# A hybrid retention, sparse attention and mixture-of-experts layer on one core: GpSimd's order in the expert loop

## The chip, the cores and the metric

The kernel runs on one core of one Trainium2 chip. The metric is the device time in microseconds of one execution.

## The reference, cut to what matters

One layer over 512 tokens of width 1024: RMS norm with an adaptive scale and shift, a projection, retention, sparse attention with its top-k choice, an output projection, and then the mixture of experts with which this change deals:

```python
top_vals, top_idx = lax.top_k(logits, TOP_K)              # 4 of 32 experts for each of 512 tokens
gates = jax.nn.softmax(top_vals, axis=-1)
xs = h[rows_tok]                                          # rows of each block's tokens, 128 a block
gu = xb @ w_gu[e] + b_gu[e]                               # 1024 -> 2048
gate, up = jnp.split(gu, 2, axis=-1)
gate = jnp.minimum(gate, 7.0); up = jnp.clip(up, -7.0, 7.0)
glu = gate * jax.nn.sigmoid(1.702 * gate)
ys = ((up + 1.0) * glu) @ w_down[e] + b_down[e]           # 1024 -> 1024
y = segment_sum(ys * gates, rows_tok)                     # back to the tokens
```

All tensors are float32. The weights of one expert are 8 MB (w_gu) and 4 MB (w_down). Of 128 rows in an expert's block some 64 are filled on average (512 x 4 / 32); an empty row has an index out of bounds, and the indirect DMA leaves it out.

## The kernel before

**Before the loop** the normed rows are stored to DRAM (`xn_rows`), and lists are made of which token (`tok_i`) and which output row (`dst_i`) stands in each place of each expert's block, one column per expert.

**The expert loop** has 32 items and runs on five engines at once, each with its own program and its own `Fori`; they meet by semaphores. It is pipelined by one item: period `i` (a round of `steady(i)`) does gate and up of expert `i` and then down of expert `i-1`.

- SyncE loads the weights in 12 chunks of 1 MB a period into a ring of six slots. It waits for a slot until `lo_ready` says that VectorE has read it.
- ScalarE rounds each chunk to a high part (`e_hi`, four buffers), VectorE subtracts to get the low part (`e_lo`, four buffers). A product is three matmuls: high by high, low by high, high by low. ScalarE waits for `chunk_used` of TensorE before it takes a buffer of e_hi anew.
- TensorE, in `steady(i)`: `act_turn` transposes the activations of expert i-1 (L1288), `gate_up` puts down the biases (L1299) and then 8 chunks of 12 matmuls (L1306 to L1308), then it waits for `gathered`, `x_turn` transposes the gathered rows of expert i+1 out of `xg` (L1280), and `down` does the bias (L1316) and 4 chunks of 12 (L1328 to L1330).
- After x_turn, ScalarE scales and splits the transposed rows (`x_parts`, L706 and L703), between chunks. VectorE clips gate and up (L1695, L1696), makes the product (L1700, L1703), the low part of the rows (L1475), and goes on with e_lo (L1468) of the next item. ScalarE writes the result of `down` to `ys` (`rows_out`, L703 `area<-bank`).
- GpSimd does what needs indices. `gather()` brings rows of `xn_rows` into `xg` (L629, one buffer); an indirect DMA scatters `ys` to `expert_rows` (L661). Each takes its indices from a column copied first (L647 to `gidx`, L659 to `sidx`). Two more small copies choose the row of biases for gate and up (`sel_g`) and for down (`sel_d`), both L634.

**GpSimd's order in period i**, which is written by hand: `bring(i)` waits until x_turn of item i is done and gather i has landed, gathers i+1, waits for `g_bias_used`, copies sel_g. `store(i)` waits for `d_bias_used`, copies sel_d, waits for ys (`y_ready`), scatters, and waits until that scatter has landed. So gather i+1 of period i is issued after the scatter at the end of round i-1, which is early in TensorE's period i.

An indirect DMA issued from GpSimd, the loads from SyncE: they are two queues, over the same 16 DMA engines. In the profile a tile `area` is a large buffer with many views in it: xg, ys, xgT and the activations among them. `xn_rows` is the DRAM tensor of normed rows.

**After the loop** an `If` handles blocks of more than 128 rows as further items, and then the rows are read back and summed with their gates.

Of the kernel before, what the change touches and what calls it, by code (L numbers as in the profile page):

```python
# [14 lines left out]
I32 = mybir.dt.int32  # L15
U32 = mybir.dt.uint32

P = 128
# [9 lines left out]
E = 32  # L28
# [67 lines left out]
def build(nc, x, c, ada_w, ada_b, norm1_g, w_in, mix_scale, w_o, norm2_g, router_w, router_b,  # L96
# [11 lines left out]
    with ctx:  # L108
        def sb(name, shape, dt=F32):
            return ctx.enter_context(nc.sbuf_tensor(name, shape, dt))  # L110

        def sem(name):
            return ctx.enter_context(nc.semaphore(name))
# [80 lines left out]
        after = dist[:, P:2 * P]  # L194
# [34 lines left out]
        sel_g, sel_d = sb("sel_g", [96, P], BF16), sb("sel_d", [96, P], BF16)  # L229
        gidx = sb("gidx", [P, 1], U32)  # L230
# [23 lines left out]
        g_vals, g_bias = ring[0:1, 4 * SLOT:5 * SLOT], ring[0:1, 5 * SLOT:6 * SLOT]  # L254


        routes = sb("routes", [P, 1728])
        hot = routes[:, 0:512].rearrange("p (n e) -> p n e", e=E)
        hotC = routes[:, 512:640].rearrange("p (n e) -> p n e", e=E)
        hot32 = routes[:, 1024:1152].rearrange("p (t e) -> p t e", e=E)  # L260
        tabT = routes[:, 1280:1408]
        tab = routes[:, 1408:1536]
        dstf, empty = routes[:, 1536:1584], routes[:, 1584:1632]
        dst_i, tok_i = routes[:, 1632:1680].bitcast(I32), routes[:, 1680:1728].bitcast(I32)

        consts_ready, late_consts = sem("consts_ready"), sem("late_consts")
        small_in, key_in, query_in = sem("small_in"), sem("key_in"), [sem("query_in0"), sem("query_in1")]
# [34 lines left out]
        gidx_ready, gathered = sem("gidx_ready"), sem("gathered")  # L302
        sidx_ready, scattered = sem("sidx_ready"), sem("scattered")
        sel_g_ready, sel_d_ready = sem("sel_g_ready"), sem("sel_d_ready")
        g_bias_used, d_bias_used = sem("g_bias_used"), sem("d_bias_used")
        xt_full, xt_taken, at_full = sem("xt_full"), sem("xt_taken"), sem("at_full")
# [238 lines left out]
        def _(pool):  # L545
# [82 lines left out]
            def gather():  # L628
                pool.indirect_dma_start(out=xg, out_offset=None, in_=xn2_dram,  # L629
                                        in_offset=bass.IndirectOffsetOnAxis(ap=gidx[:, 0:1], axis=0),  # L630
                                        bounds_check=last_token, oob_is_err=False).then_inc(gathered, 16)

            def choose_bias(sel, at, ready):
                pool.tensor_copy(sel[:], hot96[:, at].broadcast_to((96, P))).then_inc(ready, 1)  # L634

            pool.tensor_copy(gidx[:].bitcast(I32), tok_i[:, 0:1]).then_inc(gidx_ready, 1)
            pool.wait_ge(gidx_ready, 1)
            gather()
            pool.sem_clear(gidx_ready)
            choose_bias(sel_g, slice(0, 1), sel_g_ready)  # L640
            choose_bias(sel_d, slice(0, 1), sel_d_ready)

            def bring(i, nxt):

                pool.wait_ge(xt_full, i * 2 + 2)
                pool.wait_ge(gathered, i * 16 + 16)
                pool.tensor_copy(gidx[:].bitcast(I32), tok_i[:, nxt]).then_inc(gidx_ready, 1)  # L647
                pool.wait_ge(gidx_ready, 1)
                gather()
                pool.sem_clear(gidx_ready)  # L650
                pool.wait_ge(g_bias_used, i + 1)
                choose_bias(sel_g, nxt, sel_g_ready)

            def store(i, before, now):

                pool.wait_ge(d_bias_used, i)
                choose_bias(sel_d, now, sel_d_ready)
                pool.wait_ge(y_ready, i + 1)
                pool.tensor_copy(sidx[:].bitcast(I32), dst_i[:, before]).then_inc(sidx_ready, 1)  # L659
                pool.wait_ge(sidx_ready, 1)  # L660
                pool.indirect_dma_start(out=y_dram,  # L661
                                        out_offset=bass.IndirectOffsetOnAxis(ap=sidx[:, 0:1], axis=0),
                                        in_=ys, in_offset=None,
                                        bounds_check=last_row, oob_is_err=False).then_inc(scattered, 16)
                pool.sem_clear(sidx_ready)
                pool.wait_ge(scattered, i * 16)

            def opening(i):
                bring(i, slice(i + 1, i + 2))

            def steady(i):
                nxt, before, now = pool.snap(i + 1), pool.snap(i - 1), pool.snap(i + 0)
                bring(i, bass.ds(nxt, 1))
                store(i, bass.ds(before, 1), bass.ds(now, 1))

            def closing(i):
                store(i, slice(i - 1, i), slice(i, i + 1))

            opening(0)
            with pool.Fori(1, E) as i:  # L680
                steady(i)
            closing(E)
            n_over = pool.value_load(over_i[0:1, 16:17], min_val=0, max_val=OVER)
            with pool.If(n_over > 0):
                opening(E)
                with pool.Fori(E + 1, ITEMS) as i:
                    steady(i)
                closing(ITEMS)
# [4 lines left out]
        def _(a):  # L693
            steps = [0]

            def done(ins):

                steps[0] += 1
                ins.then_inc(act_step, 1)
                a.wait_ge(act_step, steps[0])  # L700
# [191 lines left out]
            def hi(period, c):  # L892

                a.wait_ge(*period.landed(c))
                if period.i is not first or c >= PARTS:
                    a.wait_ge(chunk_used, period.at(c) - (PARTS - 1))
                copy(e_hi[:, c % PARTS, :], raw(period.raw_slot(c))).then_inc(hi_ready, 1)

            def x_parts(i):

                for half in range(2):
                    a.wait_ge(xt_full, i * 2 + (half + 1))
                    for q in range(4):
                        k = 4 * half + q
                        last = affine(xgT[:, k, :], bank[6 + half][:, q * P:(q + 1) * P], a2[:, k:k + 1],
                                      modB[:, k:k + 1])
                    last.then_inc(xt_taken, 1)
                    a.wait_ge(xt_taken, i * 2 + (half + 1))
                    copy(x_hi[:, 4 * half:4 * half + 4, :], xgT[:, 4 * half:4 * half + 4, :]).then_inc(xhi_ready, 1)

            def act_parts(i):

                for half in range(2):
                    a.wait_ge(at_full, i * 2 + (half - 1))
                    copy(act_hi[:, 4 * half:4 * half + 4, :],
                         bank[6 + half].rearrange("p (k n) -> p k n", k=4)).then_inc(ahi_ready, 1)

            def sigmoid(i):
                a.wait_ge(gate_ready, i + 1)
                nc.scalar.activation(sg, gc, ACT.Sigmoid, scale=ALPHA).then_inc(sig_ready, 1)  # L920

            def rows_out():
                copy(ys, banks[:, 2048:3072]).then_inc(y_ready, 1)
# [3 lines left out]
            def opening(i):  # L927
                period, after = Opening(i), Later(i + 1)
                for c in range(PARTS, GU):
                    hi(period, c)  # L930
                sigmoid(i)
                x_parts(i + 1)
                for c in range(PARTS):
                    hi(after, c)

            def steady(i):
                period, after = Later(i), Later(i + 1)
                act_parts(i)
                for c in range(PARTS, CHUNKS):
                    hi(period, c)  # L940
                sigmoid(i)
                x_parts(i + 1)
                for c in range(3):
                    hi(after, c)
                a.wait_ge(chunk_used, i * CHUNKS + 8)
                a.wait_ge(sel_g_ready, i + 2)
                rows_out()
                hi(after, 3)

# [12 lines left out]
            nc.scalar.activation(gates[:], dgate[:], ACT.Exp).then_inc(gate_exp, 1)  # L962
            a.wait_ge(tables_ready, 1)
            opening(0)
            with a.Fori(1, E) as i:
                steady(i)
            closing(E)
            first = None
# [1 line left out]
            with a.If(n_over > 0):  # L970
                for c in range(PARTS):
                    hi(Opening(E), c)
                opening(E)
                with a.Fori(E + 1, ITEMS) as i:
                    steady(i)
                closing(ITEMS)
# [814 lines left out]
```

## Time and profile before

| what | value |
|---|---|
| median of 3 runs | 1724.37 us (1715.86, 1724.37, 1729.37) |
| the profiled execution | 1720.0 us, span 1718.2 us |
| TensorE busy | 1583.8 us (92%) |
| VectorE busy | 1386.1 us (81%) |
| ScalarE busy | 1130.4 us (66%) |
| GpSimd busy | 335.1 us (20%) |
| DMA | 478.98 MB, mean 279 GB/s |
| the chain that ended last | PE 48%, DMA 20%, DVE 11%, ACT 11%, issue 7%, POOL 3% |
| in it | DMA expert_rows<-area,sidx 10%, DMA area<-xn_rows,gidx 8% |

PE is TensorE, DVE is VectorE, ACT is ScalarE, POOL is GpSimd, SP is SyncE. The chain is followed back from the last instruction to what released each step, so its shares are time on the path, whereas the busy times of engines overlap. The matmuls are pipelined and a matmul's duration overlaps with its neighbours'; their rate is read from the starts.

### The profile page before, as it was taken

Reading aid. Unit: us, or ns where it says so; the run is one execution under the profiler, and the core shown is the slowest. Engines: PE = TensorE matmul, PEld = TensorE weight load, DVE = VectorE, ACT = ScalarE, POOL = GpSimd, SP = SyncE. Lnnn points to the kernel's source line nnn. Section 1 sums busy time; section 2 is a strip of 40 time slices with the busy share of each in tenths; the row PEclk is TensorE's granted clock in tenths of the full one; section 3 lists DMA queues with packets and bytes.
Section 4 is the critical chain, followed back from the end, with each engine's and each line's share of the span. In section 5 each row is a group of like instructions: output and inputs, shape, how many; then the busy total and the mean of one; then the engine's idle time right before and its main releaser. Section 6 shows DMA issues by size and latency. Waiting matters only on the chain.

```text
span 1718.2 us, 20912 instructions
## 1 busy us (share of the span) xinstructions
PE 1583.8 (92%) x7032; PEld 1244.9 (72%) x7032; DVE 1386.1 (81%) x1162; ACT 1130.4 (66%) x1173; POOL 335.1 (20%) x258
## 2 busy tenths in 40 slices
PE   3999989998699999999999999999999999999975
PEld 3678866745577878778787877878787787878762
DVE  4789934246589889898988989898898989889865
ACT  3544343324487877787787777788777778878751
POOL 1215200010102212221221222122223222211210
PEclk8999985597789999999999999999999999999997
DMA  9745210023578898998889999888989998898826
GB/s 350 229 141 201 98 62 1 0 80 123 211 298 334 333 358 347 352 357 344 324 338 359 344 362 355 350 330 335 363 340 364 350 349 335 342 346 340 347 106 254
DMA packets 97712, 478.98 MB, mean 279 GB/s; under 512 B 24264, under 2 KB 33584, under 8 KB 45360
## 3 DMA queue, kind: packets, MB, share of 16 engines
q1 hardware_dynamic: 86848, 456.76, 69.8%
q0 software_dynamic: 10832, 21.81, 3.5%
q8 instruction: 18, 0.29, 0.1%
q14 instruction: 14, 0.11, 0.0%
HBM read 474.84 MB, written 20.98 MB: 289 GB/s over the span
## 4 chain that ended last, share of the span: by engine, by line
PE 48%; DMA 20%; DVE 11%; ACT 11%; issue 7%; POOL 3%; POOLq 0%; ACTq 0%; SPq 0%; DVEq 0%
DMA expert_rows<-area,sidx 10%; DMA area<-xn_rows,gidx 8%; PE bank L1307 6%; PE bank L1306 6%; PE bank L1308 6%; ACT e_hi L703 5%; PE bank L1328 4%; PE bank L1329 4%; PE bank L1330 4%; ACT area L706 3%; PE bank L1190 2%; PE bank L1135 2%; POOL sidx L659 2%; PE bank L1156 2%; DVE w_lo L1429 1%
## 5 line engine op out<-in xcount | busy, mean ns | idle before, releaser
L1468 DVE TENSOR_TENSOR e_lo<-ring,e_hi 128x2048 fp32r<-128x2048 f32 x384 | 872.5, 2293 | 120.6 <-ACT e_hi L703 117.8
L703 ACT ACTIVATE e_hi<-ring 128x2048 fp32r<-128x2048 f32 x384 | 732.7, 1920 | 218.9 <-PE bank L1308 198.9
L1306 PE MATMUL bank<-e_hi,x_hi 128*128 128x512 f32 x1024 | 407.5, 398 | 1.5 <-DVE e_lo L1468 1.5
L1307 PE MATMUL bank<-e_lo,x_hi 128*128 128x512 f32 x1024 | 404.0, 395 | 0.0
L1308 PE MATMUL bank<-e_hi,x_lo 128*128 128x512 f32 x1024 | 402.8, 393 | 0.0
L1306 PEld LDWEIGHTS bank<-e_hi,x_hi 128*128 128x128 f32 x1024 | 193.5, 189 | 48.5 <-DVE e_lo L1468 2.4
L1307 PEld LDWEIGHTS bank<-e_lo,x_hi 128*128 128x128 f32 x1024 | 193.4, 189 | 42.1
L1308 PEld LDWEIGHTS bank<-e_hi,x_lo 128*128 128x128 f32 x1024 | 193.2, 189 | 41.6
L1328 PE MATMUL bank<-e_hi,act_hi 128*128 128x512 f32 x512 | 210.8, 412 | 4.9 <-DVE act_lo L1481 4.9
L1329 PE MATMUL bank<-e_lo,act_hi 128*128 128x512 f32 x512 | 203.8, 398 | 0.0
L1330 PE MATMUL bank<-e_hi,act_lo 128*128 128x512 f32 x512 | 203.3, 397 | 0.0
L703 ACT ACTIVATE area<-bank 128x1024 f32<-128x1024 f32 (+5 forms) x90 | 59.9, 665 | 153.0 <-PE bank L1023 68.0
L1328 PEld LDWEIGHTS bank<-e_hi,act_hi 128*128 128x128 f32 x512 | 97.5, 191 | 31.4 <-DVE act_lo L1481 5.4
L1330 PEld LDWEIGHTS bank<-e_hi,act_lo 128*128 128x128 f32 x512 | 97.4, 190 | 23.6
L1329 PEld LDWEIGHTS bank<-e_lo,act_hi 128*128 128x128 f32 x512 | 97.6, 191 | 22.7
L706 ACT ACTIVATE area<-bank,modB,a 128x128 f32<-128x128 f32 x264 | 98.4, 452 | 18.8 <-PE bank L1280 18.7
L659 POOL COPY sidx<-routes 128x1 int32 (+1 forms) x32 | 37.5, 1172 | 374.3 <-ACT area L703 374.3
L634 POOL COPY sel_d<-hot 96x128 bf16 (+1 forms) x33 | 32.2, 976 | 313.1 <-PE bank L1316 310.7
L647 POOL COPY gidx<-routes 128x1 int32 (+1 forms) x32 | 39.7, 1241 | 258.9 <-DMA expert_rows<-area,sidx 230.4
L1280 PE MATMUL bank<-ident,area 128*128 128x128 f32 x264 | 37.7, 289 | 41.3 <-DMA area<-xn_rows,gidx 41.3
L578 POOL TENSOR_TENSOR area<-ring,area 128x2048 f32<-128x2048 f32 x10 | 48.5, 4859 | 134.8 <-ACT ring L703 127.5
L1280 PEld LDWEIGHTS bank<-ident,area 128*128 128x128 f32 x264 | 31.8, 148 | 50.2 <-issue 43.4
(245 smaller groups left out, 1996.2 us busy)
## 6 DMA issues: line engine op xcount, KB each, us to landing
ring<-in_w_gu SPq DMA_DIRECT2D x256, 1024.0 KB, 6.4
ring<-in_w_down SPq DMA_DIRECT2D x128, 1024.0 KB, 6.9
ring<-in_ada_w SPq DMA_DIRECT2D x24, 1024.0 KB, 7.3
ring<-in_w_in SPq DMA_DIRECT2D x9, 1024.0 KB, 6.1
ring<-expert_rows SPq DMA_DIRECT2D x6, 1024.0 KB, 10.7
ring<-in_w_o SPq DMA_DIRECT2D x4, 1024.0 KB, 7.4
ring<-in_w_in SPq DMA_DIRECT2D x10, 256.0 KB, 5.2
xs<-in_x SPq DMA_DIRECT2D x4, 512.0 KB, 5.1
```

Of the source, the lines that this page charges most:

```text
L578: nc.gpsimd.tensor_tensor(o, slot(LOAD_B[n]), o, ALU.add).then_inc(rest_used[half], 1)
L659: pool.tensor_copy(sidx[:].bitcast(I32), dst_i[:, before]).then_inc(sidx_ready, 1)
L703: return nc.scalar.activation(dst, src, ACT.Copy, scale=scale)
L706: return nc.scalar.activation(dst, src, ACT.Identity, scale=scale, bias=bias)
L1280: mm = pe.transpose(bank[6 + half][:, q * P:(q + 1) * P], xg[:, k * P:(k + 1) * P], ident[:])
L1306: pe.matmul(bank[b][:], x_hi[:, c, :], hi, start=False, stop=False)
L1307: pe.matmul(bank[b][:], x_hi[:, c, :], lo, start=False, stop=False)
L1308: mm = pe.matmul(bank[b][:], x_lo[:, c, :], hi, start=False, stop=(c == GU - 1))
L1328: pe.matmul(bank[4 + q][:], act_hi[:, kk, :], hi, start=False, stop=False)
L1329: pe.matmul(bank[4 + q][:], act_hi[:, kk, :], lo, start=False, stop=False)
L1330: mm = pe.matmul(bank[4 + q][:], act_lo[:, kk, :], hi, start=False, stop=(kk == KD - 1))
L1468: tt(e_lo[c % PARTS][:], raw(period.raw_slot(c)), e_hi[:, c % PARTS, :].bitcast(F32), ALU.subtract).then_inc(lo_ready, 1)
```

## The change

In GpSimd's program the gather of an item is put behind the transposes that empty `xg`: round i now chooses sel_g, waits for x_turn of item i+1, and gathers item i+2; the first two gathers stand before the loop. The wait for a landed scatter at the end of `store` goes; GpSimd waits for the scatter before only where it overwrites `sidx`, and ScalarE waits for it before it overwrites `ys` (where it waited for sel_g). Since the last rounds read two columns ahead, the list of tokens has eight more columns, which are set to zero before the first gather. The first round is written out on GpSimd and ScalarE, as it has no scatter to wait for.

```diff
-        routes = sb("routes", [P, 1728])
+        routes = sb("routes", [P, 1736])
...
-        dst_i, tok_i = routes[:, 1632:1680].bitcast(I32), routes[:, 1680:1728].bitcast(I32)
+        dst_i, tok_i = routes[:, 1632:1680].bitcast(I32), routes[:, 1680:1736].bitcast(I32)
...
-            pool.tensor_copy(gidx[:].bitcast(I32), tok_i[:, 0:1]).then_inc(gidx_ready, 1)
-            pool.wait_ge(gidx_ready, 1)
-            gather()
-            pool.sem_clear(gidx_ready)
-            choose_bias(sel_g, slice(0, 1), sel_g_ready)
-            choose_bias(sel_d, slice(0, 1), sel_d_ready)
-
-            def bring(i, nxt):
-
-                pool.wait_ge(xt_full, i * 2 + 2)
-                pool.wait_ge(gathered, i * 16 + 16)
+            done(nc.gpsimd.memset(tok_i[:, 48:56], 0))
+
+            def take_rows(nxt):
+
                 pool.tensor_copy(gidx[:].bitcast(I32), tok_i[:, nxt]).then_inc(gidx_ready, 1)
                 pool.wait_ge(gidx_ready, 1)
                 gather()
                 pool.sem_clear(gidx_ready)
+
+            take_rows(slice(0, 1))
+            choose_bias(sel_g, slice(0, 1), sel_g_ready)
+            choose_bias(sel_d, slice(0, 1), sel_d_ready)
+            pool.wait_ge(xt_full, 2)
+            pool.wait_ge(gathered, 16)
+            take_rows(slice(1, 2))
+
+            def bring(i, nxt, after):
+
                 pool.wait_ge(g_bias_used, i + 1)
                 choose_bias(sel_g, nxt, sel_g_ready)
+                pool.wait_ge(xt_full, i * 2 + 4)
+                pool.wait_ge(gathered, i * 16 + 32)
+                take_rows(after)
 
             def store(i, before, now):
 
                 pool.wait_ge(d_bias_used, i)
                 choose_bias(sel_d, now, sel_d_ready)
                 pool.wait_ge(y_ready, i + 1)
+                if i is not 1:
+                    pool.wait_ge(scattered, (i - 1) * 16)
                 pool.tensor_copy(sidx[:].bitcast(I32), dst_i[:, before]).then_inc(sidx_ready, 1)
...
                 pool.sem_clear(sidx_ready)
-                pool.wait_ge(scattered, i * 16)
 
             def opening(i):
-                bring(i, slice(i + 1, i + 2))
+                bring(i, slice(i + 1, i + 2), slice(i + 2, i + 3))
 
             def steady(i):
-                nxt, before, now = pool.snap(i + 1), pool.snap(i - 1), pool.snap(i + 0)
-                bring(i, bass.ds(nxt, 1))
+                if i is 1:
+                    bring(1, slice(2, 3), slice(3, 4))
+                    store(1, slice(0, 1), slice(1, 2))
+                    return
+                after, nxt = pool.snap(i + 2), pool.snap(i + 1)
+                before, now = pool.snap(i - 1), pool.snap(i + 0)
+                bring(i, bass.ds(nxt, 1), bass.ds(after, 1))
                 store(i, bass.ds(before, 1), bass.ds(now, 1))
 
             def closing(i):
                 store(i, slice(i - 1, i), slice(i, i + 1))
+                pool.wait_ge(scattered, i * 16)
 
             opening(0)
-            with pool.Fori(1, E) as i:
+            steady(1)
+            with pool.Fori(2, E) as i:
                 steady(i)
...
                 a.wait_ge(chunk_used, i * CHUNKS + 8)
-                a.wait_ge(sel_g_ready, i + 2)
+                if i is not 1:
+                    a.wait_ge(scattered, (i - 1) * 16)
                 rows_out()
                 hi(after, 3)
...
             opening(0)
-            with a.Fori(1, E) as i:
+            steady(1)
+            with a.Fori(2, E) as i:
                 steady(i)
```

## Rows read from the trace of the kernel before

**Rows 1.** Busy times by stretch: length, busy of each engine, PEclk, DMA share, GB/s.

```profile
516.50:1651.70 1135.20, 1098.16 (x4982) 890.86 (x4981) 1025.35 (x601) 893.75 (x781) 249.97 (x180) 0.99 0.89 344
896.10:935.20 39.10, 36.52 (x168) 29.50 (x167) 36.62 (x22) 30.80 (x27) 10.47 (x6) 1.00 0.90 357
935.20:971.50 36.30, 36.30 (x168) 29.58 (x167) 31.75 (x20) 28.82 (x26) 6.91 (x6) 1.00 0.91 339
```

**Rows 2.** Waits, 516.5 to 1651.7: total us, times, longest.

```profile
POOL gidx L647 <- DMA expert_rows<-area,sidx: 230.4, 30, 9.2
ACT e_hi L703 <- PE bank L1308: 183.8, 225, 0.9
...
PE bank L1280 <- DMA area<-xn_rows,gidx: 37.0, 15, 2.8
```

**Rows 3.** The chain, 896 to 923: start, us, what.

```profile
896.93 1.02 ACT area L703
898.10 2.09 POOL sidx L659
900.48 11.13 DMA expert_rows<-area,sidx
912.20 1.26 POOL gidx L647
913.73 8.78 DMA area<-xn_rows,gidx
```

**Rows 4.** TensorE's timeline at four places: start, us, what, idle before.

```profile
922.63 1.09 PE L1280 MATMUL bank<-ident,area 128*128 128x128 f32 x8 [2.58 <-DMA area<-xn_rows,gidx]
...
958.98 1.04 PE L1280 MATMUL bank<-ident,area 128*128 128x128 f32 x8
...
971.45 1.11 PE L1288 MATMUL bank<-ident,area 128*128 128x128 f32 x8
...
973.08 0.59 PE L1306 MATMUL bank<-e_hi,x_hi 128*128 128x512 f32 x1
```

**Rows 5.** Busy times by stretch, two of four with PEclk at 0.50.

```profile
543.10:546.50 3.40, 3.32 (x12) 2.80 (x13) 3.40 (x4) 3.19 (x7) 0.35 (x1) 0.50 1.01 424
...
1526.10:1529.50 3.40, 3.40 (x10) 2.63 (x9) 3.37 (x3) 3.34 (x10) 1.89 (x1) 0.50 1.09 414
```

**Rows 6.** The gathers of L629, from issue to landing.

```profile
DMA to landing us min/median/max: 4.3/8.5/10.5
```

**Rows 7.** VectorE's timeline from 968.85.

```profile
968.85 6.70 DVE L1468 TENSOR_TENSOR e_lo<-ring,e_hi 128x2048 fp32r<-128x2048 f32 x3
```

**Rows 8.** DMA, 516.5 to 1651.7: all, and the instruction queue.

```profile
DMA packets 60193, 390.72 MB, mean 344 GB/s; under 512 B 10637, under 2 KB 10637, under 8 KB 14368
...
q14 instruction: 1, 0.01, 0.0%
```

**Rows 9.** Busy times by stretch, two with the DMA queues loaded.

```profile
898.00:930.00 32.00, 29.41 (x133) 23.81 (x132) 29.80 (x19) 25.26 (x24) 10.47 (x6) 1.00 1.00 404
934.00:964.00 30.00, 30.00 (x140) 24.50 (x139) 25.35 (x15) 21.88 (x18) 6.91 (x6) 1.00 0.97 363
```

**Rows 10.** Waits of SyncE's DMA queue, 516.5 to 1651.7.

```profile
SPq L478 <- DVE e_lo L1468: 629.3, 233, 6.3
```

**Rows 11.** GpSimd's timeline at the first gather.

```profile
428.79 0.18 POOL L636 COPY gidx<-routes 128x1 int32<-128x1 int32 x1 [18.89 <-DVE routes L1661]
429.56 2.95 POOL L629 DMA_INDIRECT area<-xn_rows,gidx  x1 [0.59 <-POOL gidx L636]
```

**Rows 12.** GpSimd's groups before 480: busy us, mean ns, idle before.

```profile
L615 POOL MEMSET area<- 128x1024 f32 x1 | 1.0, 970 | 0.0
```

**Rows 13.** GpSimd's groups, 516.5 to 1651.7.

```profile
L629 POOL DMA_INDIRECT area<-xn_rows,gidx x30 | 40.7, 1357 | 9.2 <-POOL gidx L647 9.2
L647 POOL COPY gidx<-routes 128x1 int32 x30 | 38.8, 1295 | 230.4 <-DMA expert_rows<-area,sidx 230.4
```

**Rows 14.** All instructions of VectorE's line 1468: ns min/median/max.

```profile
L1468 DVE TENSOR_TENSOR e_lo<-ring,e_hi x384: 2278/2292/2378, 429.2 to 1655.7; 128x2048 fp32r<-128x2048 f32 x192
```

## The prediction

> **What bounds the kernel now.** I read the stretches first, then the waits, then the chain, then single timelines. The expert loop from period 2 to period 31 takes 1135.20 of the 1718.2 us span [rows 1]. A period here runs from one transposition of the activations (L1288) to the next; there are 30 of them in that stretch, 37.84 us each on average. They are not alike. The third row of [rows 1] is one in which TensorE is busy all 36.30 us. The second is its neighbour: 39.10 us with the same 168 matmuls and 36.52 us busy. So a period of 36.30 us is what TensorE itself needs at full clock, and everything over it is waiting.
>
> The waits say on whom [rows 2]. In these 30 periods TensorE has one kind of wait only: the transposes of the next expert's rows (L1280) wait for the gather, 15 times, 37.0 us in all. It waits for no e_lo and no DMA of weights there. ScalarE waits for TensorE (183.8 us over 225 times, to get an e_hi buffer back), and the GpSimd queue has 230.4 us of waiting for a scatter to land before it copies the next indices.
>
> The chain through one slow period gives the order [rows 3]. ys is written at 896.93, GpSimd copies the scatter's indices (2.09 us), the scatter takes 11.13 us from its issue to its landing, the loop's last line waits for it, then come the copy of the gather's indices and the gather itself, 8.78 us. It lands at 922.5, and the transposes start at 922.63, 2.58 us late [rows 4]. The gather needs nothing of the scatter: its buffer xg was emptied by the transposes one period earlier. It stands behind it only in GpSimd's program. In the other period of a pair scatter and gather are quicker and the transposes (958.98) start without any wait [rows 4]. That is why it is 15 of 30.
>
> A stall costs twice where the clock falls. [...] At half speed 3.4 us hold 1.7 us of work: 4 x 1.7 = 6.8 us.
>
> **The change part by part.**
>
> *The gather moves to right behind the transposes.* In period i, GpSimd now waits for the transposes of rows i+1 (the end of L1280), copies indices and gathers rows i+2. Those are read by the transposes of the next period. From rows: transposes end at 960.0 (958.98 + 1.04) [rows 4]; the index copy is at most about 2.1 us (the sidx copy of [rows 3], nearest of its size), and a gather landed 4.3 to 10.5 us after its issue [rows 6]. That gives landing at most 13 us after the transposes, and it is wanted 36.30 - 1.04 = 35.3 us after. Some 22 us are to spare, so no ordinary delay brings the wait back. What goes: 30 x 36.30 = 1089.0 us in place of 1135.20, that is **-46.2 us**. The terms agree: 37.0 us of waits, 6.8 us of clock, and 2.4 us left, 0.16 for each of the 15 stalls, the start of PE's pipeline after a stop.
>
> *The scatter's wait moves to its users.* ScalarE waits for scatter i-1 before it writes ys, and GpSimd before it overwrites sidx. That scatter was issued at about 4 us into the period and landed by 16 us (900.48 + 11.13, against 896.1) [rows 3]; ys is next written at 36.30 + 0.8 us. 20 us to spare: 0 us. ScalarE loses its wait for sel_g, which never ended last in [rows 2]: 0 us. If the gather in the same queue held the scatter up by a whole gather (10.5 us), 9 us would still be left.
>
> *GpSimd's queue.* Per period it issues what it did: four small copies and two indirect DMAs. Behind its new wait for the transposes stand the gather, sel_d, and the scatter. sel_d is wanted by `down` of the next period, 30 us later; the scatter's ys comes 12 us after the transposes (971.45 against 958.98) [rows 4], while gather issue plus copies are 2.1 + 3.0 + 2.1 us at the most. sel_g is chosen before the wait, about 7 us into the period, wanted at its end. 0 us.
>
> *What is late next.* The chain of the next expert's first e_lo. In the period without a wait VectorE makes e_lo of the next chunks 0 to 2 in one run from 968.85, 2.23 us each [rows 7], so chunk 0 is there at 971.1; the matmul that reads it starts at 973.08 [rows 4]. Margin 2.0 us. That period has this margin already at full pace, and its neighbours met it too, so two in a row need nothing new. VectorE works 1025.35 us in the stretch [rows 1], 34.2 per period, 94% of 36.30: near, not over.
>
> *The transfers.* The stretch moves 390.72 MB [rows 8]. In 1089.0 us that is 359 GB/s, now 344. Over 32 us the same queues moved 404 GB/s at a share of 1.00, and in the period without a wait 363 GB/s at 0.97, which is 374 at a full share [rows 9]. 359 is under both. SP's queue waits for e_lo to free a slot 233 times with 629.3 us for w_gu alone [rows 10]: loads are held back by slots, not by the engines. Cost 0, cover about 4% in the worse of the two rows.
>
> *Before the loop.* A memset of 128x8 with a wait of its own comes between the ready lists and the first gather, which is on the path (TensorE waits for that gather). There GpSimd took 0.18 us for a copy of that size and 0.59 us to the next [rows 11]; a memset of 128x1024 took 0.97 us [rows 12]. Between 0.2 and 2.1 us (a copy that met VectorE, [rows 3]); I take **+0.6 us**, as the short copy and a wait are nearest. Once more GpSimd gathers at the very end (34 gathers for 33), for a list that is not used; nothing waits for it: 0 us. The peeled first rounds on GpSimd and ScalarE lengthen the code and repeat no work. The instruction queue moved one packet in all 30 periods [rows 8], so a loop's code is not fetched anew each round: 0 us, at most the 2.1 us of a short stall, once.
>
> **Sum.** 1720.0 (the profiled execution, span 1718.2) - 46.2 + 0.6 = 1674.4 us. The profiled execution is 4.4 us below the median of 1724.37. If that difference is in the stalls, it goes with them; if it is elsewhere, it stays (1678.8). I say 1675.
>
> **Rivals.**
>
> *GpSimd gets in VectorE's way (1694).* The copy of the indices (mean 1.30 us) and the gather's issue (1.36 us) [rows 13] now fall beside VectorE's clip, swiglu and x_lo, the chain with 2.0 us of margin. Were VectorE held for both, 2.66 - 2.0 = 0.66 us are lost per period; 30 x 0.66 = 20, so 1694. (Over 2.0 + 1.54 us of holding a period, 1.54 being 46.2 / 30, the gain would be gone.) Against it: the longest of 384 e_lo instructions took 2378 ns with a median of 2292 [rows 14], though GpSimd's copies and issues fell beside many of them. It is GpSimd that waits: its copies of one column take 0.18 or 2.09 us [rows 3, 11]. [...] I give this 5%.
>
> *The transfers don't keep up (slower, 1737).* With no stalls left, the ring of six slots gets no periods in which to catch up, and gather and scatter lie close together: one in the last 10 us of a period, the other in the first 14. If the queues then deliver only 339 GB/s, which is what the period without a wait shows as a whole [rows 1], a period takes 13.02 MB / 339 = 38.4 us, 2.1 more, and the whole 1674.4 + 63 = 1737. It decides from 344 GB/s down, where all the gain is gone, and below 338 (a period of 38.55 us) the time is over 1742. For it: 339 there, and share 0.91. Against: that row includes time in which SP had no free slot, and where the queues had work they gave 363 to 404. 5%.
>
> *Nothing changes (1720).* The transposes would have to be held by something that merely ends with the gather, or the clock would fall without stalls. [rows 2] names the gather in all 15, and [rows 5] are all at a wait. 5%.
>
> **The numbers.** The forecast has 83%, the three rivals 15%, other things 2%. A measurement of this kernel tells about 1% from no change, 1707 to 1742. Faster by over 1%: 0.83 + 0.05 (VectorE held) + 0.02 = 0.90. Within 1%: 0.05 from nothing changes and 0.02 from transfers between 338 and 350 GB/s, 0.07. Slower: 0.03, transfers below 338. The low end is the sum less the spread of the runs (1715.86 against 1724.37 is 8.5): 1666. The high end takes in 1678.8 and the VectorE case: 1695.
>
> **What would show it.** In the profile after: no wait of L1280 for the gather between periods 2 and 31, periods of 36.30 us throughout, granted clock 1.00 over that stretch, its length 1089 us, DMA share about 0.93. GpSimd's idle time before the gidx copy is ended by TensorE (L1280), not by the scatter. Wrong would be: an idle before L1306 ended by e_lo (the margin of 2.0 us is gone), ScalarE's e_hi waiting for a DMA (transfers), ys waiting for the scatter, or half-clock stretches inside the loop without a stall.

## The result: 1675.68 us, as forecast, and the profile after

The changed kernel takes 1675.68 us (median of 4 runs, 1674.71 to 1678.61) against 1726.87 us for the kernel before on the same chip: a ratio of 0.9694, interval 0.9651 to 0.9736. A run over 1.5% above the fastest of its kernel counts as slow: two runs of the kernel before do in the later sessions, two of the version held to 5 chunks (experiment 2) and one of that held to 6. The profiled execution is 1675.41 us with a span of 1673.6 us. Forecast: 1675, range 1666 to 1695.

The stretches, from the first transposition of period 2 to that of period 32, and one period (length, busy of PE, PEld, DVE, ACT, POOL, granted clock, DMA share, GB/s):

```profile
518.50:1607.50 1089.00, 1089.00 (x4982) 887.31 (x4981) 1020.04 (x601) 888.78 (x781) 255.47 (x180) 1.00 0.91 359
881.50:917.80 36.30, 36.30 (x168) 29.58 (x167) 34.00 (x21) 29.62 (x27) 8.51 (x6) 1.00 0.93 363
```

Against [rows 1]: 1089.00 us for 1135.20, TensorE busy all of it, the clock at 1.00 throughout. All 30 periods are 36.30 us, where there were 15 of 36.3 and 15 of 38.7 to 40.8. The DMA share is 0.91, where the prediction looked for 0.93. The waits of that stretch (total us, times, longest):

```profile
POOL gidx L640 <- PE bank L1296: 478.8, 30, 16.0
POOL sidx L667 <- ACT area L717: 338.0, 30, 11.3
ACT e_hi L717 <- PE bank L1324: 174.0, 210, 0.9
DVE e_lo L1484 <- ACT e_hi L717: 63.7, 150, 0.5
```

TensorE is in no row. The 230.4 us in which GpSimd waited for its scatter before a gather [rows 2] are now 478.8 us in which it waits for the transposes: more idle time than before, and none of it on the path. The chain that ended last says the same by shares:

```profile
PE 84%; DVE 9%; ACT 3%; DMA 2%; issue 1%; SPq 0%; DVEq 0%; POOLq 0%; POOL 0%; ACTq 0%
```

It was PE 48% and DMA 20%; the two indirect DMAs (10% and 8%) have gone out of it. GpSimd's timeline of one period, which begins at 881.5 (start, us, what, idle before):

```profile
883.59 2.01 POOL L667 COPY sidx<-routes 128x1 int32 x1 [11.28 <-ACT area L717]
885.87 2.77 POOL L669 DMA_INDIRECT expert_rows<-area,sidx  x1 [0.28 <-POOL sidx L667]
888.65 1.97 POOL L634 COPY sel_g<-hot 96x128 bf16 x1
906.57 0.42 POOL L640 COPY gidx<-routes 128x1 int32 x1 [15.96 <-PE bank L1296]
907.26 1.04 POOL L629 DMA_INDIRECT area<-xn_rows,gidx  x1 [0.27 <-POOL gidx L640]
908.31 0.30 POOL L634 COPY sel_d<-hot 96x128 bf16 x1
```

The gather is issued 25.8 us into the period and is wanted 34 us later, since the transposes stand 23.8 us into the next one (958.98 against 935.20 in [rows 1, 4]). It takes 3.8 to 8.6 us to land, where it took 4.3 to 10.5 [rows 6]:

```profile
DMA to landing us min/median/max: 3.8/7.5/8.6
```

What is outside the loop: the first gather. The last step of the list before it, in the chain of before and of after, and then GpSimd's timeline after:

```profile
428.31 0.19 DVE routes L1661
```

```profile
430.06 0.19 DVE routes L1677
```

```profile
430.50 0.10 POOL L636 MEMSET routes<- 128x8 int32 x1 [18.85 <-DVE routes L1677]
430.67 0.18 POOL L640 COPY gidx<-routes 128x1 int32<-128x1 int32 x1
431.32 2.94 POOL L629 DMA_INDIRECT area<-xn_rows,gidx  x1 [0.46 <-POOL gidx L640]
```

The list was ready 1.75 us later in this execution, before any changed instruction (and 5.43 us later, at 433.93, in the one of experiment 6). From the end of that step to the gather's issue it is 1.07 us (430.25 to 431.32), with the memset's 0.10 in it, and before it was 1.06 (428.50 to the 429.56 of [rows 11]).

### The profile page after: what moved, and what is told of

It is laid out like the page before. It is cut to its first block, busy times and chain, and to the rows that moved or that the text cites. A ratio compares the mean times of both kernels' runs of the same rounds, so it can differ in the third digit from the quotient of the medians.

```text
span 1673.6 us, 20929 instructions
## 1 busy us (share of the span) xinstructions
PE 1574.7 (94%) x7032; PEld 1241.6 (74%) x7032; DVE 1379.7 (82%) x1162; ACT 1125.2 (67%) x1173; POOL 343.2 (21%) x261
## 4 chain that ended last, share of the span: by engine, by line
PE 84%; DVE 9%; ACT 3%; DMA 2%; issue 1%; SPq 0%; DVEq 0%; POOLq 0%; POOL 0%; ACTq 0%
PE bank L1323 14%; PE bank L1324 14%; PE bank L1322 14%; PE bank L1344 7%; PE bank L1346 7%; PE bank L1345 7%; PE bank L1206 3%; PE bank L1151 2%; PE bank L1172 2%; PE bank L1304 2%; PE bank L1315 2%; PE bank L1296 2%; DVE w_lo L1445 2%; DMA ring<-in_ada_w 1%; PE bank L1159 1%; PE bank L1037 1%
## 5 line engine op out<-in xcount | busy, mean ns | idle before, releaser
L1323 PE MATMUL bank<-e_lo,x_hi 128*128 128x512 f32 x1024 | 404.1, 395 | 0.0
L1323 PEld LDWEIGHTS bank<-e_lo,x_hi 128*128 128x128 f32 x1024 | 193.4, 189 | 42.2
L667 POOL COPY sidx<-routes 128x1 int32 (+1 forms) x32 | 62.6, 1956 | 364.2 <-ACT area L717 364.2
L640 POOL COPY gidx<-routes 128x1 int32 (+1 forms) x34 | 14.2, 418 | 533.2 <-PE bank L1296 533.1
L669 POOL DMA_INDIRECT expert_rows<-area,sidx x32 | 86.8, 2713 | 9.0 <-POOL sidx L667 9.0
L634 POOL COPY sel_g<-hot 96x128 bf16 (+1 forms) x33 | 62.9, 1906 | 11.1 <-PE bank L1315 11.0
L1560 DVE SCALAR_TENSOR_TENSOR area<-area,bank 128x128 f32<-128x128 f32 (+3 forms) x32 | 15.6, 487 | 51.5 <-PE bank L1151 51.5
```

What stands on the lines that cost most here:

```text
L669: pool.indirect_dma_start(out=y_dram, out_offset=bass.IndirectOffsetOnAxis(ap=sidx[:, 0:1], axis=0), in_=ys, in_offset=None, bounds_check= ...
L1323: pe.matmul(bank[b][:], x_hi[:, c, :], lo, start=False, stop=False)
```

## The experiments

All were timed in 3 rounds against the kernel before on the same chip, whose medians were 1727.67, 1725.28 and 1724.28 us in the three sessions. Each edit is shown against the changed kernel.

**1. Which half of the change did it.** The gather moved, the scatter's wait kept where it was:

```diff
                 pool.sem_clear(sidx_ready)
+                pool.wait_ge(scattered, i * 16)
```

> The changed kernel, but GpSimd still waits at the end of each round for its scatter to land. Theory (the gather was late only because it stood behind the scatter): the wait now ends about 15.5 us into the period, before sel_g (wanted at 36) and before the transposes of the next rows (25), so nothing moves: 1675 us, all 30 periods 36.30. Rival (the removed scatter wait was the real cause): back to 1720.

1676.77 us, ratio 0.9709 (0.9655 to 0.9764). The rival falls. GpSimd does wait for its scatter again, 30 times, but now before sel_g, where nobody is waiting:

```profile
POOL sel_g L634 <- DMA expert_rows<-area,sidx: 256.7, 30, 9.4
```

So 256.7 us of waiting for a scatter cost nothing in this place of the program, whereas 230.4 us of such waiting [rows 2] stood in front of the gather before.

The other half alone: the gather stays in its old place, behind the scatter's issue, and only the wait between them is gone.

```diff
-            pool.wait_ge(xt_full, 2)
-            pool.wait_ge(gathered, 16)
-            take_rows(slice(1, 2))
...
             def bring(i, nxt, after):
 
+                pool.wait_ge(xt_full, i * 2 + 2)
+                pool.wait_ge(gathered, i * 16 + 16)
+                take_rows(nxt)
                 pool.wait_ge(g_bias_used, i + 1)
                 choose_bias(sel_g, nxt, sel_g_ready)
-                pool.wait_ge(xt_full, i * 2 + 4)
-                pool.wait_ge(gathered, i * 16 + 32)
-                take_rows(after)
```

> Only the scatter's wait is moved; the gather keeps its old place, right behind the scatter's issue in GpSimd's program. Theory: scatter issued by 7.2 us into the period, index copy up to 2.1, gather issued at about 9.5 and landed 7.5 to 10.5 later, 17 to 20 us, wanted at 23.8: no wait either, 1675 us. Rival (the gather has to stand behind the transposes; two indirect DMAs of one queue follow each other whole): the gather starts when the scatter has landed, as before, and the time stays at 1720.

1673.94 us, ratio 0.9693 (0.9639 to 0.9748): the whole gain again. GpSimd's timeline, in a period that begins at 877.8 (start, us, what, idle before):

```profile
879.95 2.00 POOL L664 COPY sidx<-routes 128x1 int32 x1 [12.68 <-ACT area L714]
882.23 2.77 POOL L666 DMA_INDIRECT expert_rows<-area,sidx  x1 [0.28 <-POOL sidx L664]
885.00 1.87 POOL L640 COPY gidx<-routes 128x1 int32 x1
887.14 1.04 POOL L629 DMA_INDIRECT area<-xn_rows,gidx  x1 [0.27 <-POOL gidx L640]
```

and the gathers' time from issue to landing:

```profile
DMA to landing us min/median/max: 4.3/9.7/10.7
```

The gather is issued at 9.3 us, behind a scatter in flight, and lands by 20.0 at the latest, 3.8 before it is wanted at 23.8. Either half is enough; the two do not add.

**2. How late may the gather be.** From the version just shown, the gather is also held until gate and up of the current expert have used 3, 5 or 6 chunks (the line for 5):

```diff
                 pool.wait_ge(gathered, i * 16 + 16)
+                if i is not 0:
+                    pool.wait_ge(chunk_used, i * CHUNKS + 1)
                 take_rows(nxt)
```

> The gather held until gate and up have used 3 chunks, 10.2 us into the period. Theory (36.30 plus what the landing is later than 23.8): lands at 10.3 + 1.4 + 0.3 + 8.3 = 20.3 on the mean and at 22.3 with the longest landing seen (10.7): 1675 us, no wait. With the runs held to chunks 5 and 6 that makes a knee between. Rival (holding GpSimd's program behind chunks costs by itself): over 1700.

> As the run with the wait moved only, and the gather is held until gate and up of the current expert have used 5 chunks, 15.8 us into the period. Theory (a period costs 36.30 plus what the landing is later than 23.8): copy 0.4 to 2.1, 0.3, landing 7.5: 24.0 to 25.7, so 0.2 to 1.9 us of wait, 0.16 for the restart, 31 times: 1686 to 1739, middle 1712. Rival (the gather isn't what counts): 1675.

> As before, held to 6 chunks, 18.6 us into the period: 2.79 us more in each of 31 periods, so 86 us over the run held to chunk 5 if the clock stays (about 1798), and up to 1.7 x 31 = 53 us on top if the granted clock falls at every wait (about 1850). A slope of less than 2.79 us a period would say that something else than the gather's landing ends the wait.

Held to 3: 1675.72 us, ratio 0.9728 (0.9701 to 0.9754), all periods 36.30. Held to 5: 1768.97 us (1740.40 to 1787.08), ratio 1.0272 (1.0191 to 1.0353), above the range of 1686 to 1739. Against the kernel before that leaves open whether it is slower by over 2%. Against the same version without the hold, timed in the same session (experiment 1, second half, 1671.52 to 1678.36), every run is at least 62 us longer. Held to 6: 1889.95 us (1875.22 to 1903.95), ratio 1.0912 (1.0810 to 1.1015), above the 1850. The knee is where it was expected, the loss behind it is larger. TensorE's waits in the 30 periods, first held to 5, then to 6:

```profile
PE bank L1295 <- DMA area<-xn_rows,gidx: 50.6, 25, 3.5
```

```profile
PE bank L1295 <- DMA area<-xn_rows,gidx: 131.5, 30, 5.9
```

and the loop's stretches, in the same order:

```profile
514.90:1673.40 1158.50, 1107.81 (x4982) 894.96 (x4982) 1024.46 (x600) 895.63 (x780) 221.24 (x180) 0.99 0.88 336
```

```profile
528.30:1817.00 1288.70, 1157.18 (x4985) 933.02 (x4985) 1033.02 (x601) 904.46 (x781) 178.54 (x180) 0.94 0.81 302
```

Held to 6, the 30 gaps before the transposes are 4.4 us each, close to the 4.8 that 18.6 + 1.4 + 0.3 + 8.3 - 23.8 gives, and 2.7 us more than held to 5, where 2.79 was expected. So the gather's landing ends the wait, as the theory says. What the expectation had too small is the clock. It was at 0.50 in 29 pieces, 160 us together, which is up to 80 us of lost work (part of it lies in the gaps, where nothing is lost twice); gaps and clock together make the 199 us over 1089. The expectation had one piece of 3.4 us a wait at the most, the length of those in [rows 5]; 18 of the 29 were of 6.8. Held to 5, gaps of 51 us and half of the 31 us at a granted clock of 0.50 make 66 of the 69 over 1089, and 0.16 for each of 25 waits about the rest (what the 0.16 is stands with the loop's term below). That expectation's range held no term for the clock. All this is the profiled execution, the fastest of four at 1740.40; no trace shows where the other three lost up to 47 us more.

**3. VectorE's margin.** One or two more products of 128x1024 behind swiglu, ahead of x_lo and the next e_lo; their result is not used (the lines for two; the semaphore's declaration is left out).

```diff
                 tt(act, uc, sg, ALU.mult).then_inc(act_ready, 1)
+                for k in range(2):
+                    tt(uc, uc, sg, ALU.mult).then_inc(more_ready, 1)
+                    v.wait_ge(more_ready, i * 2 + (k + 1))
```

> The changed kernel with one more 128x1024 product on VectorE per item, behind swiglu, in the chain that makes the next item's first e_lo (its result is not used). Theory (that chain has 2.0 us of margin): 1.23 us and some 0.1 for its own wait fit in, 36.30 us a period, 1675 us. Rival (VectorE at 94% of the period is as good as full): 1.3 us a period, 31 x 1.3 = 40, 1715 us.

> The same with two more products, 2.6 us. Theory: 0.6 us over the margin in each of 31 periods, 19 us: 1694 us, with TensorE's wait before L1322 ended by e_lo; if these waits make the granted clock fall, up to 1.7 us each on top. Rival (full already): 31 x 2.6 = 81, 1756 us.

One: 1674.64 us, ratio 0.9689 (0.9625 to 0.9754), periods 36.30. Two: 1690.72 us, ratio 0.9785 (0.9719 to 0.9850), periods of 36.74 with one gap, before the first L1323, ended by e_lo:

```profile
PEld bank L1323 <- DVE e_lo L1485: 18.7, 29, 0.6
```

0.44 us a period where 0.6 was expected, and 30 x 0.44 = 13 of the 16 us between the two medians. So the margin is 2.1 to 2.2 us, near the 2.0 read from [rows 4, 7], and the granted clock stayed at 1.00 with these waits. VectorE was busy 1067.50 of 1087.00 us there:

```profile
520.00:1607.00 1087.00, 1082.63 (x4910) 872.87 (x4909) 1067.50 (x650) 874.57 (x764) 241.48 (x176) 1.00 0.89 357
```

98% busy cost 0.44 us a period, and 97% with one product none. Here the busy share did not say when VectorE begins to hold others up; the margin in one chain did.

**4. GpSimd beside VectorE.** Four copies of 128x512 behind each gather's issue:

```diff
                 gather()
                 pool.sem_clear(gidx_ready)
+                for k in range(4):
+                    pool.tensor_copy(future[:], dist[:]).then_inc(gidx_ready, 1)
+                    pool.wait_ge(gidx_ready, k + 1)
+                pool.sem_clear(gidx_ready)
```

> The changed kernel with four copies of 128x512 on GpSimd right behind each gather's issue, SBUF to SBUF, beside VectorE's clip, swiglu, x_lo and e_lo. Theory (GpSimd is the one that waits): each copy takes up to 2.3 us in the trace, VectorE's e_lo stays at 2291 ns median and under 2400, the time at 1675 us. [...]

1674.73 us, ratio 0.9684 (0.9619 to 0.9748): no time lost. But the theory's sentence that VectorE is untouched is wrong: the longest e_lo in the 30 periods took 2643 ns. GpSimd's four copies in one period (start, us, what):

```profile
909.67 0.62 POOL L645 COPY future<-dist 128x512 f32<-128x512 f32 x1
```

```profile
910.36 0.61 POOL L645 COPY future<-dist 128x512 f32<-128x512 f32 x1
```

```profile
911.04 2.55 POOL L645 COPY future<-dist 128x512 f32<-128x512 f32 x1
```

```profile
913.65 1.49 POOL L645 COPY future<-dist 128x512 f32<-128x512 f32 x1
```

VectorE's timeline beside them:

```profile
909.36 1.22 DVE L1716 TENSOR_SCALAR area<-bank 128x1024 f32<-128x1024 f32 x1
910.49 2.63 DVE L1488 TENSOR_TENSOR e_lo<-ring,e_hi 128x2048 fp32r<-128x2048 f32 x1
913.04 1.62 DVE L1720 SCALAR_TENSOR_TENSOR area<-area 128x1024 f32<-128x1024 f32 x1
914.70 1.52 DVE L1723 TENSOR_TENSOR area<-area 128x1024 f32<-128x1024 f32 x1
```

and the same four without them, in the changed kernel:

```profile
908.00 1.21 DVE L1712 TENSOR_SCALAR area<-bank 128x1024 f32<-128x1024 f32 x1
909.13 2.28 DVE L1484 TENSOR_TENSOR e_lo<-ring,e_hi 128x2048 fp32r<-128x2048 f32 x1
911.33 1.22 DVE L1716 SCALAR_TENSOR_TENSOR area<-area 128x1024 f32<-128x1024 f32 x1
912.58 1.23 DVE L1719 TENSOR_TENSOR area<-area 128x1024 f32<-128x1024 f32 x1
```

The three instructions with two inputs in SBUF (e_lo and the two products) are 0.3 to 0.4 us longer each, 1.0 us together, less than the margin of 2.1. On the mean of 30 periods the two products take 1.63 and 1.52 us against 1.22 and 1.23. The clip, which reads a bank, is as long as before, and the copies beside it take 0.61 and 0.62 us, near the 568 ns of an iota of that size. The third copy begins while e_lo runs and ends at 913.59, 0.47 us behind the end of e_lo (913.12); the fourth ends 0.48 us behind the end of the first product (914.66). So of the 2.55 and 1.49 us that they took, all but 0.47 and 0.48 lie beside VectorE's instruction, where a whole copy took 0.61 beside the clip. The other way round, each of the three VectorE instructions began 0.44 to 0.55 us before the end of a copy that was running, and is longer by a little less than that. In these five meetings both sides were held: what came second took longer by about the time that the other still ran. That VectorE can be held by GpSimd, as the prediction's rival has it, is shown here, and with it how little it costs: three VectorE instructions of a period met a copy, and each lost 0.3 to 0.4 us, what was left of the copy and not all of it.

**5. The transfers' margin.** One or two more loads of 1 MB a period in SyncE's queue, to a spare DRAM tensor that nobody reads (the line for two):

```diff
                     gu_chunk(period, c, e)
+                    if c in (3, 6):
+                        sp.dma_start(spare[i, (c % 2) * P:(c % 2 + 1) * P, :], w_gu[e, c * P:(c + 1) * P, :]).then_inc(spare_in, 16)
```

> The changed kernel with one more load of 1 MB per period in SyncE's queue, from w_gu to a spare DRAM tensor (not used). 14.06 MB a period, 387 GB/s at 36.30 us. Theory (the queues can do 374 to 404 at a full share): between no loss (404) and 37.6 us a period (374), so 1675 to 1715, middle 1690. Rival (the transfers were already the limit at 359): 13.02 to 14.06 MB is 8% of 36.30, 2.9 us a period, 31 x 2.9 = 90, 1765.

> The same with 2 MB more, 15.1 MB a period, 416 GB/s at 36.30 us, over both rows. Theory: the queues bound the period, 15.1 MB / 404 = 37.4 us to 15.1 / 374 = 40.4: 31 x 1.1 to 4.1 = 34 to 127 more, 1709 to 1802, and ScalarE's e_hi waits for a DMA. Rival (limit already at 359): 42.1 us a period, 1855.

One: 1677.25 us, ratio 0.9738 (0.9716 to 0.9759), periods of 36.30. Two: 1697.11 us, ratio 0.9848 (0.9824 to 0.9871), below the range. All the DMA of 520 to 1607, with one and with two:

```profile
DMA packets 61113, 420.81 MB, mean 387 GB/s; under 512 B 11161, under 2 KB 11161, under 8 KB 14835
```

```profile
DMA packets 61039, 445.81 MB, mean 410 GB/s; under 512 B 11395, under 2 KB 11395, under 8 KB 15069
```

and with two, ScalarE's waits and the loads' median time to landing (6.8 us in the changed kernel):

```profile
ACT e_hi L721 <- DMA ring<-in_w_gu: 108.1, 31, 4.6
ACT e_hi L721 <- DMA ring<-in_w_down: 54.7, 96, 0.9
```

```profile
ring<-in_w_gu SPq DMA_DIRECT2D x234, 1024.0 KB, 11.6
```

The limit is a little above the better of the expectation's two rows (404): 410 GB/s at a share of 0.99, and 15.1 MB / 410 = 36.9 us against the 37.0 us that the periods take from the ninth on; periods 2 to 8 still take 36.30. So the changed kernel has a cover of 410 / 359, 14%, not 4%. The extra loads go from DRAM to DRAM; whether loads into SBUF alone reach 410 is not shown.

**6. The memset.** Put ahead of the wait for the lists:

```diff
+            done(nc.gpsimd.memset(tok_i[:, 48:56], 0))
             pool.wait_ge(xn2_stored, 16 * T)
             pool.wait_ge(lists_ready, 1)
...
-            done(nc.gpsimd.memset(tok_i[:, 48:56], 0))
```

> The changed kernel with the memset of the eight new columns put ahead of the wait for the lists. Both theories: within the noise in time (1675 us). In the trace the memset (0.10 us and about 0.07 to the copy behind it) leaves the path to the first gather: gidx copy 0.2 us sooner after the list is ready than the 0.27 us shown with the memset. The 0.6 us of the prediction for it would be too much.

1675.68 us, ratio 0.9688 (0.9623 to 0.9753). GpSimd's timeline there:

```profile
434.23 0.18 POOL L640 COPY gidx<-routes 128x1 int32<-128x1 int32 x1 [18.79 <-DVE routes L1677]
435.00 2.93 POOL L630 DMA_INDIRECT area<-xn_rows,gidx  x1 [0.58 <-POOL gidx L640]
```

and the last step of the list in the same run:

```profile
433.74 0.19 DVE routes L1677
```

From the end of that step to the copy it takes 0.30 us, and 0.42 with the memset in between (430.25 to 430.67): 0.12 sooner, where 0.2 was expected. To the gather's issue it is 1.07 us either way, so the memset costs the gather nothing. The medians show no version faster than the changed kernel by more than the spread of its runs.

## Why the prediction was right

**What bounds it.** Right. The 15 waits for the gather (37.0 us [rows 2]), with a granted clock of 0.50 for 3.4 us behind each of four of them [rows 5] (from about 543, 847, 1526 and 1601 us), were what stood over 36.30 us, and moving the gather's landing in three steps moved the time with it, with a knee between 3 and 5 chunks (experiment 2).

**The loop, -46.2 us.** 1135.20 - 1089.00 = 46.20, measured. The terms of the kernel before add up to it: 37.0 us of waits, 4 x 1.7 = 6.8 us for the clock, and 15 x 0.16 = 2.4. The 0.16, which the prediction put down to the start of PE's pipeline, is how the profile counts a wait. The last matmuls before the wait of 2.58 us in [rows 4] (start, us, what):

```profile
919.42 0.40 PE L1307 MATMUL bank<-e_lo,x_hi 128*128 128x512 f32 x1
919.65 0.39 PE L1308 MATMUL bank<-e_hi,x_lo 128*128 128x512 f32 x1
```

They start 0.23 us apart and last 0.39 to 0.40, and a wait is counted from the end of the last, so some 0.16 us more than the wait is lost. That a period without a wait can follow another was argued from its margin, and it does.

**The scatter's wait, 0.** Right as said: scatter and ys need nothing sooner. What the prediction did not see is that this part alone would have brought the whole gain (experiment 1). It priced the two parts as a cause (the gather's place) and a thing without cost (the wait), where either is enough.

**The front, +0.6.** The mis-sized term: 0.01 us by the trace (1.07 against 1.06). The size was taken from a copy and the 0.59 us behind it; that gap stands before the issue of the indirect DMA in the kernel before too [rows 11], and was 0.46 after. The 2.1 us that the prediction allowed once for a short stall by the longer code is its author's guess: no run shows such a stall, and the 30 periods of 36.30 us hold none.

**The sum.** Span: 1718.2 - 46.2 + 2.0 - 0.4 = 1673.6. Of the 2.0, 1.75 came before the changed code, and the 0.4 lies behind the loop. With the 1.8 between span and time that is the 1675.41 measured. The forecast of 1674.4 is 1.0 off: the drifts of 2.0 and 0.4, less the 0.6 that the front did not cost. The kernel before stood 4.4 us over its profiled execution by the median of three runs and 6.9 by that of four, so the gain by the medians is 51 us, not 46. That excess did not come back: the changed kernel's median is 0.3 above its profiled run. The spread of the runs went the same way. In the session of the result the kernel before ranges over 22 us and the changed kernel over 4; the other versions without a wait for the gather in the loop range over 4 to 9. That the waits make the spread is likely by this, but no trace shows it.

**VectorE held by GpSimd.** Did not decide, as forecast; its argument was half wrong. The 2378 ns maximum of e_lo [rows 14] was read as "GpSimd is the one that waits". With copies of 512 columns VectorE is held as well, 0.3 to 0.4 us at each meeting (experiment 4). A copy of one column is over after 0.18 us where nothing holds it [rows 11], so there is little of it left to be held for; that this is why the maximum was low is argued, not tried. The rival's 1694 was priced wrong too, in the safe direction. The 1.30 and 1.36 us of [rows 13] were taken as times for which VectorE could be held, but a GpSimd duration holds its own standing still (0.61 against 2.55 us for the same copy). In the changed kernel the longest e_lo took 2375 ns, so next to nothing of the margin of 2.0 us was needed.

**The transfers.** Did not decide. The 363 GB/s at a share of 0.97 [rows 9] was turned into a capacity of 374, which is too low: at a share of 0.99 over 1087 us the same engines moved 410 (experiment 5). The better row, 404 at 1.00, was near it. Why the 363 stood so low was not tried.

**Why only every other period waited before.** Read, not tried. In the period after a wait, GpSimd's part ran quicker (start, us, what, idle before):

```profile
936.62 0.25 POOL L659 COPY sidx<-routes 128x1 int32 x1 [10.44 <-ACT area L703]
937.32 1.02 POOL L661 DMA_INDIRECT expert_rows<-area,sidx  x1 [0.46 <-POOL sidx L659]
```

The copy took 2.09 us in the slow period and the scatter 11.13 from issue to landing [rows 3]; here the scatter landed in under 7. VectorE had nothing to do from 936.82 to 938.29, as it waited for ScalarE's e_hi, so the copy and the issue hardly met it. The loads were not out of the way: the DMA engines moved 362 GB/s at a share of 0.96 during this scatter, against 396 at 0.99 during the slow one. How much each of the two gave is open.

## What to carry to other kernels

Where one queue holds transfers of two kinds, write down for each when its buffer comes free and when its result is wanted, and issue it right behind the first; a wait for a landing holds up all that stands behind it in its engine's program, whether it needs that landing or not (here 230.4 us of GpSimd's time before the gathers of 30 periods). Before a stall is taken away, read the margin of what comes next in a stretch that has no stall: such a stretch is the best model of the kernel after. Take the capacity of the transfers from a stretch in which the DMA share is at 1 (here 404 GB/s, where 410 was reached later, and not the 374 from a share of 0.97), and an engine's limit from the margin of its chain (2.1 to 2.2 us of VectorE), not from its busy share (97% cost nothing). Do not price what an engine does to its neighbour by a duration that holds its own standing still (2.55 us for a copy of 0.61).

## What the runs showed of the hardware

- Two indirect DMAs in one GpSimd queue overlap from issue to landing: a gather issued 4.9 us behind a scatter (10.9 us to its landing by the median) landed in 9.7 us (median), against 8.5 us behind a wait for that scatter and 7.5 us in the changed kernel.
- In the kernel before, a wait of TensorE of 2.2 to 2.8 us was followed by a granted clock of 0.50 for 3.4 us in 4 of 15 cases; in the version held to 6 chunks gaps of 2.2 to 5.9 us, 4.4 on the mean, brought 29 such pieces in 30 periods (160 us), 18 of them of 6.8 us. Waits that made a period 0.44 us longer (two products) or 0.7 to 1.2 us longer (two loads) brought none (clock 1.00).
- The core's 16 DMA engines moved 410 GB/s at a share of 0.99 over 1087 us (two loads more a period) with loads of 1 MB, two indirect DMAs a period and copies from DRAM to DRAM among them.
- A GpSimd copy of 128x512 float32 took 0.61 us beside a VectorE clip that reads a bank, and 2.55 us where it came in behind the start of an e_lo with two SBUF inputs; it ended 0.47 us behind e_lo (four copies). VectorE instructions with two SBUF inputs that began during such a copy took 0.3 to 0.4 us more.
